# S5's parameters and states of a hybrid decoder step arrive already laid out by state index

## What is computed

```python
proj = h @ w_in                              # [z | x,B,C | dt | u | gate_a | gate_b]
y_a = rms_norm(ssd(conv(xBC), dt) * silu(z)) @ w_ssm_out     # branch A, 8 head groups
# branch B: S5, 128 groups of 16 channels, one complex state of 64 per group
step = exp(log_dt)[:, None]
mag  = exp(lr * step); ar, ai = mag * cos(li * step), mag * sin(li * step)
qr, qi = ...(ar, ai, lr, li)
bbar_re = qr[..., None] * br - qi[..., None] * bi            # b: (group, state, channel)
bbar_im = qr[..., None] * bi + qi[..., None] * br
s_re, s_im = scan over the tokens of (ar, ai, bbar @ u), from the given states
y = s_re . c_re - s_im . c_im + d_skip * u                   # c: (group, channel, state)
y_b = glu(gelu(y) @ w_glu)
x = x + rms_norm((sigmoid(g_a) * y_a + sigmoid(g_b) * y_b) @ w_out)
x = x + rms_norm(swiglu(rms_norm(x)))
return y, new ssm and conv states, s_re[-1], s_im[-1]        # final S5 states
```

## Time and profile before

| | us |
|---|---|
| median of 3 runs | 2429.34 |
| lowest, highest | 2428.74, 2429.76 |
| the profiled execution, whole | 2429.21 |
| its span in the trace | 2427.1 |
| TensorE busy | 2397.6 (99%) |
| VectorE busy | 1665.6 (69%) |
| ScalarE busy | 1081.2 (45%) |
| mean granted clock of TensorE | 0.993 of full |

### The profile page before, as it was taken

How to read it: one execution, slowest core, us unless ns; L and a number is a source line. 1 busy time by engine, 2 the same in 40 slices (tenths; PEclk the granted TensorE clock), 3 DMA queues, 4 the chain that set the end, 5 groups by cost and what they waited for, 6 DMA issues and landing times.

```text
span 2427.1 us, 50201 instructions
## 1 busy us (share of the span) xinstructions
PE 2397.6 (99%) x19379; PEld 2345.6 (97%) x19379; DVE 1665.6 (69%) x3013; ACT 1081.2 (45%) x1610; POOL 13.9 (1%) x38
## 2 busy tenths in 40 slices
PE   9999999999999989999999999999999999999998
PEld 9999999999999989999999999999999999999998
DVE  7888988979889767798956565655555555544444
ACT  6453544535445334645553334543333334333332
POOL 1000000000000000000000000000000000000000
PEclk9999999999999999999999999999999999999999
DMA  7666766667576697555686666465555555565543
GB/s 215 197 209 185 227 185 203 207 197 234 181 208 201 188 216 222 144 155 167 182 221 199 196 196 206 130 189 172 164 164 158 171 165 164 162 199 170 158 159 122
DMA packets 603144, 448.30 MB, mean 185 GB/s; under 512 B 77872, under 2 KB 584208, under 8 KB 601872
## 3 DMA queue, kind: packets, MB, share of 16 engines
q1 hardware_dynamic: 578384, 435.02, 60.7%
q10 hardware_dynamic: 24608, 11.20, 1.9%
HBM read 409.35 MB, written 36.76 MB: 184 GB/s over the span
## 4 chain that ended last, share of the span: by engine, by line
PE 92%; DVE 4%; DMA 1%; issue 1%; ACT 1%; ACTq 1%; SPq 0%; POOL 0%; DVEq 0%; POOLq 0%
PE acc L2053 28%; PE acc L2054 28%; PE acc L2055 28%; PE side L2040 2%; PE side L2139 1%; DVE w_lo L1301 1%; PE side L2212 1%; PE side L2193 1%; ACTq L956 0%; ACT w_hi L786 0%; PE side L2357 0%; PE side L2063 0%; DMA yt<-y_scratch 0%; DMA u_scratch<-uo 0%; PE side L2380 0%
## 5 line engine op out<-in xcount | busy, mean ns | idle before, releaser
L1301 DVE TENSOR_TENSOR w_lo<-raw,w_hi 128x1024 fp32r<-128x1024 f32 (+2 forms) x692 | 830.2, 1208 | 528.9 <-ACT w_hi L786 524.1
L786 ACT ACTIVATE w_hi<-raw 128x1024 fp32r<-128x1024 f32 (+2 forms) x692 | 716.1, 1044 | 919.6 <-PE acc L2055 886.1
L2053 PE MATMUL acc<-h_hi,w_hi 128*128 128x288 f32 x3472 | 1035.1, 298 | 6.7 <-DVE w_lo L1301 6.7
L2054 PE MATMUL acc<-h_lo,w_hi 128*128 128x288 f32 x3472 | 1026.7, 296 | 0.0
L2055 PE MATMUL acc<-h_hi,w_lo 128*128 128x288 f32 x3472 | 1026.7, 296 | 0.0
L2053 PEld LDWEIGHTS acc<-h_hi,w_hi 128*128 128x128 f32 x3472 | 654.1, 188 | 14.7 <-DVE w_lo L1301 7.1
L2054 PEld LDWEIGHTS acc<-h_lo,w_hi 128*128 128x128 f32 x3472 | 654.8, 189 | 1.4
L2055 PEld LDWEIGHTS acc<-h_hi,w_lo 128*128 128x128 f32 x3472 | 654.3, 188 | 0.0
L2053 PE MATMUL acc<-f_hi,w_hi 128*128 128x288 f32 x704 | 208.1, 296 | 0.0
L2055 PE MATMUL acc<-f_hi,w_lo 128*128 128x288 f32 x704 | 207.8, 295 | 0.0
L2054 PE MATMUL acc<-f_lo,w_hi 128*128 128x288 f32 x704 | 207.6, 295 | 0.0
(11 more groups left out here) (367 smaller groups left out, 2508.8 us busy)
## 6 DMA issues: line engine op xcount, KB each, us to landing
raw<-in_w_in_dram SPq DMA_DIRECT2D x512, 256.0 KB, 3.7
raw<-in_w_ffn_up_dram SPq DMA_DIRECT2D x352, 256.0 KB, 3.4
raw<-in_w_ffn_down_dram SPq DMA_DIRECT2D x160, 256.0 KB, 2.9
raw<-in_w_ssm_out_dram SPq DMA_DIRECT2D x128, 256.0 KB, 3.6
raw<-in_w_glu_dram SPq DMA_DIRECT2D x128, 256.0 KB, 3.7
h<-in_state_ssm_dram SPq DMA_DIRECT2D x32, 512.0 KB, 6.5
out_ssm_sample_dram<-h SPq DMA_DIRECT2D x32, 512.0 KB, 3.0
raw<-in_w_out_dram SPq DMA_DIRECT2D x64, 256.0 KB, 3.1
```

The lines of the kernel that those rows point to most:

```text
L786: copy = lambda out, in_, **k: nc.scalar.activation(out, in_, ACT.Copy, **k)
L1301: tt(w_lo[:, slot, 0:n], raw[:, slot, 0:n], w_hi[:, slot, 0:n].bitcast(F32), ALU.subtract).then_inc(lo_ready, 1)
L2053: mm(o_, wh, xh[:, kt, :], start=first and i == 0, stop=False)
L2054: mm(o_, wh, xl[:, kt, :], start=False, stop=False)
```

## The change

The host hands over five new arrays, `s5_lambda` (real, imaginary and log_dt), `s5_b`, `s5_c`, `state_s5` and `s5_skip` (D, already masked), each with 128 partitions first and whole rows of a partition side by side, and takes one output `s5_new` for all final states. SP issues all loads, seven DMAs in all: `lam` (96 KB), `bb5` and `ct5` in two parts each, the states, and `dd5` (512 KB each). The turns of lambda, C, states and final states are gone, their copies too, but for one: ScalarE changes the sign of C's imaginary part in place. The final states leave from `fin5` in one DMA of 128x1152 numbers (576 KB), issued by ScalarE ten steps earlier than the old stores. The diff, cut to its core:

```diff
@@ SP
             def lambda_load():
-                sp.wait_ge(sem("conv_out"), 6 * NG)
-                sp.wait_ge(sem("conv_rows"), 6 * NG)
...
+                sp.wait_ge(sem("heads_ready"), NG)
+                sp.dma_start(lam[:, :, :], a['s5_lambda']).then_inc(sem("lambda_landed"), 16)
...
-                v = a[('state_s5_re', 'state_s5_im')[k]][0].rearrange("b (g p) n -> g p b n", g=2)
-                for g2 in range(2):
-                    sp.dma_start(sn5[:, k, :, g2 * S5N:(g2 + 1) * S5N], v[g2]).then_inc(sem("s5_states_landed"), 16)
+                sp.dma_start(st5[:, 64:72, :, :], a['state_s5']).then_inc(sem("s5_states_landed"), 16)
-            def c_load(k, g2):
+            def b_load(k):
                 sp.wait_ge(sem("y2_ready"), NG)
-                wait(sp, "c_landed", 32 * k)
-                v = a[('s5_c_re', 's5_c_im')[k]][0].rearrange("(g b p) c n -> g (p c) b n", g=2, p=8)[g2]
-                sp.dma_start(cn5[:, k, :, g2 * S5N:(g2 + 1) * S5N], v).then_inc(sem("c_landed"), 16)
+                sp.dma_start(bb5[:, k], a['s5_b'][:, k]).then_inc(sem("b_landed"), 16)
+            def c_load(k):
+                sp.wait_ge(sem("h0_updated"), 8 * NG)
+                sp.dma_start(ct5[:, k], a['s5_c'][:, k]).then_inc(sem("c_landed"), 16)
...
-                if t in (25, 27):
-                    c_load(0, (t - 25) // 2)
+                if t in (18, 23):
+                    b_load((t - 18) // 5)
...
-                if z in (1, 3):
-                    c_load(1, z // 2)
-                if z in (4, 5):
-                    s5_states_load(z - 4)
+                if z in (0, 3):
+                    c_load(z // 3)
+                if z == 5:
+                    s5_states_load()
...
                 if z == SCAN0 + 3:
                     sp.wait_ge(sem("q_matrices"), 16)
...
-                            sp.dma_start(dst[:, g2], v[:, e, g2].to_broadcast([64, PAIRS // 2, S5C])).then_inc(sem("skip_landed"), 16)
+                    sp.dma_start(dd5[:, :, :], a['s5_skip']).then_inc(sem("skip_landed"), 16)
@@ ScalarE
-                    copy(lam[:, :, :], s0[:, 0:3 * PAIRS].rearrange("p (k g) -> p k g", k=3)).then_inc(sem("lam_ready"), 1)
-                if t in (28, 31):
-                    c_copies((t - 28) // 3)
-                if t == 33:
...
-                        copy(st5[:, 64:72, k, :], (s1 if k == 0 else s0)[:, :].rearrange("p (b g) -> p b g", b=DB)).then_inc(sem("s5_states_ready"), 1)
...
-            def b_load(k, g2):
-                act.wait_ge(sem("y2_ready"), NG)
-                v = a[('s5_b_re', 's5_b_im')[k]][0].rearrange("(g p) n c -> g n p c", g=2)[g2]
-                act.dma_start(bb5[g2 * S5N:(g2 + 1) * S5N, k], v).then_inc(sem("b_landed"), 16)
+                if t == 35:
+                    act.wait_ge(*reach("c_landed", 32))
+                    copy(ct5[:, 1], ct5[:, 1], scale=-1.0).then_inc(sem("c_ready"), 1)
...
-                if t in (15, 18, 21, 24):
-                    b_load((t - 15) // 6, (t - 15) // 3 % 2)
...
-                act.wait_ge(*reach("fo_copied", 5))
...
+                act.wait_ge(*reach("finals_done", 2))
+                act.dma_start(o['s5_new'], fin5[:, :, :, :]).then_inc(sem("s5_finals_stored"), 16)
...
-                if FIN0 < z <= FIN0 + 5:
-                    finals_copy(z - FIN0 - 1)
-                if z == FIN0 + 6:
+                if z == OUT0 + 13:
                     finals_store()
@@ VectorE
-            def skip_added(k):
-                if k == 0:
...
-                        last = tt(dd5[r], dd5[r], bc(ident[r, 64 * e + 48:64 * e + 64], PAIRS, 1), ALU.mult)
...
+            def skip_added():
+                dve.wait_ge(*reach("skip_landed", 16))
+                dve.wait_ge(sem("gs_ready"), 8)
+                tt(gs5[:, :, :], gs5[:, :, :], dd5[:, :, :], ALU.add).then_inc(sem("skip_added"), 1)
@@ TensorE
-                        last = turn(s0[:, k * PAIRS:(k + 1) * PAIRS], ln5[:, k, :])
...
-                    last = turn((s2 if b < 4 else s3)[:, (b % 4) * P:(b % 4 + 1) * P], cn5[:, k, b, :])
...
-                            last = turn((s1 if k == 0 else s0)[:, b * PAIRS:(b + 1) * PAIRS], sn5[:, k, b, :])
...
-                    last = turn(side[n % 4][0:PAIRS, m * P:(m + 1) * P], fin5[:, k, b, :])
@@ POOL
-            pool.wait_ge(sem("c_turned"), 4)
+            pool.wait_ge(sem("y2_ready"), NG)
```

More of the change, by code:

```diff
@@ L295, in build @@
     assert used["st5"][0] >= used["gth"][1] and used["gth"][1] >= used["abc"][0]
[L296 to L299, removed]
+    assert used["st5"][0] + 64 * 2 * PAIRS * 4 >= used["h0"][0]
     pr5, at = sb("pr5", [P, 14, PAIRS], F32, used["craw"][0])
-    ln5, at = sb("ln5", [PAIRS, 3, P], F32, at)
-    ldt, at = sb("ldt", [PAIRS, 2], F32, at)
-    assert used["ln5"][0] >= used["cacc"][0] and at <= used["cnew"][0]
+    assert at <= used["hist"][0]
     scr5, _ = sb("scr5", [P, 2, 2 * PAIRS], F32, used["cm"][0])
@@ L971, in splits @@
                 split(act_c, k + (c0 + t + LEAD) // 4, (t + LEAD) % 4)
[L973 to L976, removed]
             def s5_parameters(t):
                 if t == 9:
-                    act.wait_ge(*reach("lam_turned", 1))
-                    act.wait_ge(sem("heads_ready"), NG)
+                    act.wait_ge(*reach("lambda_landed", 16))
                     act.wait_ge(sem("z_done"), 4 * NG)
-                    copy(lam[:, :, :], s0[:, 0:3 * PAIRS].rearrange("p (k g) -> p k g", k=3)).then_inc(sem("lam_ready"), 1)
-                    act.wait_ge(*reach("lam_ready", 1))
+                    act.wait_ge(sem("conv_rows"), 6 * NG)
                     nc.scalar.activation(pr5[:, 0, :], lam[:, 2, :], ACT.Exp).then_inc(sem("s5_step"), 1)
@@ L1780, in scan_sums @@
                 tt(col(n + 1), col(n + 1), scr[0], ALU.add).then_inc(sem("scan_stepped"), 1)
-            def skip_added(k):
-                if k == 0:
-                    dve.wait_ge(*reach("skip_landed", 64))
-                    for e in range(2):
-                        r = slice(64 * e, 64 * e + 64)
-                        last = tt(dd5[r], dd5[r], bc(ident[r, 64 * e + 48:64 * e + 64], PAIRS, 1), ALU.mult)
-                    last.then_inc(sem("skip_masked"), 1)
-                else:
-                    dve.wait_ge(*reach("skip_masked", 1))
-                    dve.wait_ge(sem("gs_ready"), 8)
-                    tt(gs5[:, :, :], gs5[:, :, :], dd5[:, :, :], ALU.add).then_inc(sem("skip_added"), 1)
+            def skip_added():
+                dve.wait_ge(*reach("skip_landed", 16))
+                dve.wait_ge(sem("gs_ready"), 8)
+                tt(gs5[:, :, :], gs5[:, :, :], dd5[:, :, :], ALU.add).then_inc(sem("skip_added"), 1)
             a4i9, a4r9 = bc(po5[:, 1, 3, :], 9, 1), bc(po5[:, 0, 3, :], 9, 1)
@@ L1853, in _ @@
                     o_matrices(0, part)
-                if z in (T0 - 4, T0 - 2):
-                    skip_added((z - T0 + 4) // 2)
+                if z == T0 - 2:
+                    skip_added()
                 if z in (T0 + 6, T0 + 12):
@@ L2182, in side_work @@
                         within(s2, 1, g).then_inc(sem("y1_ready"), 1)
-                        if not conv:
-                            pe.wait_ge(*reach("lam_ready", 1))
                         within(s0, 2, g).then_inc(sem("y2_ready"), 1)
@@ L2401, in s5_out @@
                                     last.then_inc(sem("y5_product"), 1)
-            def finals_turn(n):
-                if n == 0:
-                    pe.wait_ge(*reach("finals_done", 2))
-                    pe.wait_ge(sem("s5_y_copied"), 16)
-                if n == 4:
-                    pe.wait_ge(*reach("fo_copied", 1))
-                for m in range(4 if n < 4 else 2):
-                    k, b = (4 * n + m) // 9, (4 * n + m) % 9
-                    last = turn(side[n % 4][0:PAIRS, m * P:(m + 1) * P], fin5[:, k, b, :])
-                last.then_inc(sem("s5_finals_turned"), 1)
             def s5_piece(z, kt):
@@ L2435, in s5_piece @@
                     s5_out(out_block(z))
-                if FIN0 <= z < FIN0 + 5 and kt == 1:
-                    finals_turn(z - FIN0)
             pe.wait_ge(sem("y_split"), 32)
@@ L2605 @@
     nc = _bacc.Bacc("TRN2", target_bir_lowering=False, num_devices=1)
-    given = {name: _np.asarray(inputs[name]) for name in NAMES}
+    given = {name: _np.asarray(inputs[name]) for name in NAMES if name in inputs}
     given['state_ssm'] = given['state_ssm'][0].reshape(DB, NG, HG * HD, NS).transpose(1, 3, 0, 2)
@@ L2611 @@
     given['state_conv'] = _np.concatenate(by_group, axis=2).transpose(3, 1, 2, 0)
+    raw_ = {name: _np.asarray(inputs[name])[0] for name in (
+        'state_s5_re', 'state_s5_im', 's5_lambda_re', 's5_lambda_im', 's5_log_dt', 's5_b_re', 's5_b_im', 's5_c_re', 's5_c_im', 's5_d')}
+    by_pair = lambda v: v.reshape(2, PAIRS, S5N).transpose(0, 2, 1).reshape(P, PAIRS)
+    given['s5_lambda'] = _np.stack([by_pair(raw_['s5_lambda_re']), by_pair(raw_['s5_lambda_im']),
```

(12 more changed lines are left out.)

83 lines of the change are left out of this document (15 added, 68 removed).

## The result

| | before | changed |
|---|---|---|
| median, us (6 runs each, in turns) | 2428.09 | 2415.18 |
| lowest, highest | 2426.35, 2429.76 | 2414.17, 2415.77 |
| the profiled execution, span | 2427.1 | 2412.1 |
| TensorE busy | 2397.6 | 2386.5 |

The ratio is 0.9948, with a 95% interval of 0.9939 to 0.9958: 12.9 us less, by the medians. The forecast was 12.0.

A forecast was written before the change was run, and what follows sets the result against it. TensorE, busy for 2397.6 of 2427.1 us, was taken to bound the kernel. Terms 4.15 + 6.9 + 1.9 + 1.0 - 2.0 = 11.95 us off 2429.2 gave 2417.2 us, range 2411 to 2424.

The forecast's parts named there:

- The turns, 4.15: TensorE's turns removed: C 1.74, states 1.14, lambda 0.2, final states 0.85 and 0.22; together 4.15 us gained.
- a new stop between 840 and 930 us: Sign against the prediction: TensorE stopping at a new place between 840 and 930 us would show it wrong.
- The final turns at 1.07: Final states' turns: the last six gain 0.85 and 0.22 us; the first twelve, ahead of S5's reload, count as nothing.
- The stops of u, 6.9 + 1.9: TensorE's stops near 883 us (for w_lo) and 895 us (for uo): 6.9 and 1.9 us gained, clock loss included.
- The floor under the second stop: Stop for uo: u_copy(4, 1) stands behind a split on ScalarE, so 1.76 us stay lost and 1.17 are gained.
- The half clock after it: Half clock after the stop for uo costs 1.5 us; half of that, 0.75, was counted as gained.
- The stop was to grow from 2.75 to 5.8: TensorE's stop near 1210 us, ended by S5's reload: 2.75 + 1.05 + 2.0, about 5.8 us.
- The cause of the first stop: Stop near 883 us: 9.86 us went into issuing two stores of u while B's small packets were on the way.
- Rival 1: The first stop stays, or a like one comes in 850 to 930 us, as the bytes remain: 2424.1 us, chance 0.14.
- D, 1.0: D's mask: VectorE loses 2.45 us of work ahead of the sum TensorE waited for; 1.0 us gained.
- The store, -2.0: Final states' store, moved ahead of S5's reload, delays that reload on nearly full DMA engines: 2.0 us lost.
- At nothing: Removed ScalarE copies, the sign change, POOL's earlier zeroing and SP's seven loads were counted as hidden, worth nothing.

The follow-up runs named there:

- e5: Changed kernel with 35 turns (lambda 3, C 16, states 16) put back on TensorE, result read by nobody, no copies: 2418.50 us.
- e11: Changed kernel with u_copy(4, 1) at z=0, last two GELU steps a slot later, final states' store late, six B-bar products spread from step 27: 2409.99 us.
- e6: Changed kernel with the 18 turns of the final states put back, result read by nobody: 2416.66 us.
- e8: Changed kernel with the copy u_copy(4, 1) moved to slot z=0, ahead of the split that waits for chunk z=0: 2413.50 us.
- e3: Changed kernel with B as before: four loads in 64-byte rows, issued by ScalarE at steps 15, 18, 21, 24: 2423.64 us.
- e1: Changed kernel with B in four loads of 64-byte rows at steps 15, 18, 21, 24, issued by SyncE: 2416.93 us.
- e2: Changed kernel with B's two loads in 4 KB rows issued by ScalarE at steps 15 and 21: 2416.10 us.
- e9: Changed kernel with VectorE's two products over D (its mask) put back: 2416.78 us.
- e4: Changed kernel with the final states' store ten steps later again, at slot FIN0+6: 2413.71 us.
- e7: Changed kernel with B in four loads of 64-byte rows on ScalarE, spaced at steps 14, 18, 22, 26: 2419.76 us.
- e12: Changed kernel unaltered, run again later: 2416.09 us.

## Why the prediction was right, and where its parts were not

The sum was 11.95 us; the medians gave 12.9 and 11.4. By its steps:

- **The turns, 4.15.** In stretch B 2.88 was put down; e5 gives 1.59. The step that missed is the one that took TensorE's pace for the time there. Without the turns, VectorE is last for 13 us: the six products of B-bar, and TensorE waits 1.0 us for `ya`. The prediction named a new stop between 840 and 930 us as a sign that it was wrong, and this one came, though worth only 1.0 of waiting (1.3 to 1.5 by e5 and e11). I had looked at what VectorE does around D and not here. The final turns at 1.07 agree with e6, within its noise; lambda's 0.2 can't be told.
- **The stops of u, 6.9 + 1.9.** In before's profile they were worth 11.12 - 1.59 = 9.5, against 8.8. The floor under the second stop was right (TensorE idle 1.50 in the window at 894, and e8 shows that ScalarE's order is all of it). The half clock after it was mis-sized: I counted on half of 1.5 coming back, and all did, 0.75 more. That makes the 9.5.
- Yet e3, the same edit undone, costs only 6.39 in its profile. It doesn't bring the first stop back whole. ScalarE's late `w_hi` comes 39.24 us after the landmark of stretch B (881.52), before's came after 41.69 (884.90), and TensorE's stop is shorter by as much: 1.5 us (of the 7.1 for `w_lo` in its trace 5.6 lie near 1210), against 3.9. The second is 4.6, against 2.7; together 6.1 and 6.6. TensorE's row in e3:

```profile
883.96 0.40 PE L1994 MATMUL acc<-h_hi,w_hi 128*128 128x288 f32 x1 [1.48 <-DVE w_lo L1252]
```

  The rest is clock. After this 1.5 the clock stays full; in before half clock follows both stops. Windows from 845 to 925 us, of before, of the changed kernel and of e3:

```profile
845.00:925.00 80.00, 73.42 (x525) 72.47 (x524) 54.42 (x97) 31.32 (x44) 0.20 (x1) 0.94 0.96 220
```

```profile
845.00:925.00 80.00, 77.51 (x574) 76.33 (x574) 65.76 (x110) 34.80 (x45) 0.00 (x0) 1.00 0.78 243
```

```profile
845.00:925.00 80.00, 72.89 (x527) 71.48 (x526) 59.13 (x102) 30.80 (x41) 0.00 (x0) 0.98 0.88 229
```

  A mean clock of 0.94 is 4.8 us lost in 80, one of 0.98 is 1.6: 3.2 us, and 9.5 less 6.4 is 3.1. So a hold-up of ScalarE that is 2.45 us shorter saves the clock of a whole stop. Why it was shorter in e3, with the same four loads, stays open: these are single profiles, and e3's median, 7.6 to 8.5 over the changed kernel's, lies between.
- **The cause of the first stop** was said to be B's small packets. e1 and e2 make it sharper: small packets in the queue of the engine that issues the stores. Rival 1 (the stop stays, since the bytes stay) is out: the bytes stayed (7.24 MB against 6.95 from 848 to 876 us), and the stop went. The engines' share did not stay: from 845 to 925 us it fell from 0.96 to 0.78, so the small rows had also kept the engines busier. The Trainium skill's page "DMA: Bandwidth & Descriptors", section "Issuing engines are not separate DMA queues", has another issuer save only the usually small issue time. e2 agrees (0.01 us in B). But from e3 to e1, where the issuer changes and with it the time of the loads, the median falls by 6.7 us and B by 3.81: e3's issues of u's stores, 8.53 us for two, were not small, and they were the cost. The same page's section "Queues, rings and completion order" gives SyncE and ScalarE each rings of their own on the shared engines, which fits that only the own queue's packets held ScalarE.
- **D, 1.0.** e9: 1.29 us in C, and the wait of 1.0 is back. Of this 0.91 shows between before and after, since the wait for `qc` grew from 0.2 to 0.6.
- **The store, -2.0.** e4: -1.5 to -2.4. Right in sum, wrong in place: I had put all of it on the reload. In the ten traces with the store early and issued at most 0.5 us ahead of the last write, that write of `y_scratch` took 5.61 to 6.08 us (5.80 in the changed kernel); with the store late 4.32 (before), 4.61 (e4) and 4.43 (e11). The reload took 9.29 to 10.35 early, 9.95 and 10.00 late. So the store lengthens the write, by 1.0 to 1.8 us, and on the reload nothing of it shows. In e1, where it was issued 2 us ahead of the write, the write took 4.16. The stop was to grow from 2.75 to 5.8, and was 4.2 and 5.4 in the changed kernel's two traces.
- **At nothing.** That seven DMAs on SP hold up no chunk is shown: no wait for `w_lo` before 1200 us, and e1, with far worse traffic, had none either. The sign change of C's imaginary part is on no chain.

The near agreement of the sum is thus in part luck, with errors on both sides: 1.3 too much for the turns, 0.7 too little for the stops.

## What to carry to other kernels

When an engine's issue of a DMA shows microseconds in its timeline, look at what it issued before into the same queue, and count its rows: either make the rows long or give them to another engine's queue. Each alone took away the hold-up, but in the other queue the small rows delayed what stood behind them there (the weights of e1), and only long rows cost nothing. Taking work off the bound engine is worth its time only where that engine is last with a margin: look at what the next engine does in the same steps (six products in three steps here), and spread it. And a stop behind a burst of DMAs was not cured here by reordering the engine that waits: the next thing in that queue was as late.

## What the runs showed of the hardware

- A DMA's issue on ScalarE, 0.33 to 0.39 us for one and 1.08 to 1.66 for two otherwise, took up to 3.60 for one and 8.53 to 9.86 for two, with loads in 64-byte rows ahead in the same queue, and 1.08 for two when those loads were in SyncE's queue.
- Two stores of u landed some 8.5 us after their issue with no small rows under way (changed kernel, and e1 after its rows had landed), and after 10.2 and 13.2 us with loads in 64-byte rows in their own queue (e3, e7).
- Half clock (1.2 instead of 2.4 GHz) followed the 4.2 us stop for 3 to 4 us, and more in e12, where the stop was 5.4; none followed the stop of 1.5 us in any trace. Near 1542 us some traces show such a stretch with no stop before it (the changed kernel's mean clock is 0.53 from 1542 to 1545), others, as e4's, show none: part of what makes D loose.
- Two executions of one kernel agreed within 0.01 us over the 81 us of stretch B, and differed by over 1 us in the stretch with S5's reload, where the DMA engines are full.
